# Late modulation in other groups and its sums four groups later; second half of the first modulation ahead of the first product

## The reference

```python
def adaln(cond, w, b):
    m = jax.nn.silu(cond) @ w + b
    return jnp.split(m, 6, axis=-1)

def trunk_block(x, mods, g1, g2, w1, w2, mixer):
    sh1, sc1, gt1, sh2, sc2, gt2 = mods
    mixed, ctx_tensors = mixer(modulate(rmsnorm(x, g1), sh1, sc1))
    x = x + gt1 * mixed
    hh = modulate(rmsnorm(x, g2), sh2, sc2)
    x = x + gt2 * (jnp.square(jax.nn.relu(hh @ w1)) @ w2)
    return x, ctx_tensors
```

## Time and profile before

| | us |
|---|---|
| median of 3 runs | 3748.66 |
| lowest and highest | 3743.83 to 3749.55 |
| the profiled execution | 3761.44 |
| its span, first to last instruction | 3760.1 |
| PE busy | 3568.7 (95%) |
| DVE busy | 2162.0 (57%) |
| mean granted clock of PE | 0.975 |

### The profile page before, as it was taken

How to read it: one execution, slowest core, us unless ns; L and a number is a source line. 1 busy time by engine, 2 the same in 40 slices (tenths; PEclk the granted TensorE clock), 3 DMA queues, 4 the chain that set the end, 5 groups by cost and what they waited for, 6 DMA issues and landing times. The chain is left out here.

```text
span 3760.1 us, 48494 instructions
## 1 busy us (share of the span) xinstructions
PE 3568.7 (95%) x19302; PEld 2735.7 (73%) x19302; DVE 2162.0 (57%) x3366; ACT 793.3 (21%) x1275; POOL 1072.2 (29%) x718
## 2 busy tenths in 40 slices
PE   7989999889999999999989999998899999999997
PEld 5887444447888888888868864444588888888886
DVE  6555676654656666666573247765446555455555
ACT  3111454441200000000031125544321000000003
POOL 0110577752211111111131127778231111111113
PEclk9999999999999999999999999999999999999999
DMA  6665344434112211211215454344501011111111
GB/s 233 192 206 167 81 122 113 126 100 172 51 66 53 79 58 61 79 50 69 69 56 162 157 145 108 84 129 114 186 32 57 25 44 45 34 34 45 34 34 56
DMA packets 274121, 350.50 MB, mean 93 GB/s; under 512 B 73286, under 2 KB 200472, under 8 KB 273768
## 3 DMA queue, kind: packets, MB, share of 16 engines
q1 hardware_dynamic: 240880, 332.75, 28.5%
q10 hardware_dynamic: 33016, 14.64, 1.9%
HBM read 280.00 MB, written 72.16 MB: 94 GB/s over the span
## 5 line engine op out<-in xcount | busy, mean ns | idle before, releaser
L2530 PE MATMUL bank<-h_hi,w_hi 128*128 128x512 f32 (+1 forms) x2496 | 904.8, 363 | 26.1 <-issue 10.5
L2531 PE MATMUL bank<-h_lo,w_hi 128*128 128x512 f32 (+1 forms) x2496 | 889.8, 356 | 0.0
L2532 PE MATMUL bank<-h_hi,w_lo 128*128 128x512 f32 (+1 forms) x2496 | 889.5, 356 | 0.0
L2345 DVE SCALAR_TENSOR_TENSOR xT<-bank,mods,xT 128x512 f32<-128x512 f32 (+1 forms) x816 | 534.3, 661 | 266.6 <-PE bank L2532 254.6
L2530 PE MATMUL bank<-m_hi,w_hi 128*128 128x512 f32 (+1 forms) x1536 | 554.4, 361 | 18.9 <-DVE xT L2345 18.6
L2530 PEld LDWEIGHTS bank<-h_hi,w_hi 128*128 128x128 f32 x2496 | 475.5, 190 | 102.0 <-issue 20.2
L2531 PE MATMUL bank<-m_lo,w_hi 128*128 128x512 f32 (+1 forms) x1536 | 548.2, 357 | 0.0
L2532 PE MATMUL bank<-m_hi,w_lo 128*128 128x512 f32 (+1 forms) x1536 | 548.1, 357 | 0.0
L2531 PEld LDWEIGHTS bank<-h_lo,w_hi 128*128 128x128 f32 x2496 | 475.7, 191 | 72.8 <-issue 5.3
L2532 PEld LDWEIGHTS bank<-h_hi,w_lo 128*128 128x128 f32 x2496 | 475.3, 190 | 67.8
L955 POOL TENSOR_SCALAR w_hi<-stage 128x2048 fp32r<-128x2048 f32 x90 | 174.2, 1935 | 1052.3 <-issue 527.6
(11 more groups left out here) (226 smaller groups left out, 4193.4 us busy)
## 6 DMA issues: line engine op xcount, KB each, us to landing
stage<-in_w_mlp SPq DMA_DIRECT2D x64, 1024.0 KB, 5.2
nx_w<-in_w_ada SPq DMA_DIRECT2D x16, 1536.0 KB, 9.4
stage<-in_w_in SPq DMA_DIRECT2D x18, 1024.0 KB, 6.2
late_w<-in_w_ada SPq DMA_DIRECT2D x32, 512.0 KB, 4.7
rope_t<-in_k_rope SPq DMA_DIRECT2D x28, 512.0 KB, 5.0
rden<-s_rden ACTq DMA_DIRECT2D x28, 320.0 KB, 4.6
ada_w<-in_w_ada SPq DMA_DIRECT2D x4, 2048.0 KB
stage<-in_w_out SPq DMA_DIRECT2D x8, 1024.0 KB, 6.4
```

What stands on the lines that cost most here:

```text
L2345: dve.scalar_tensor_tensor(out=x, in0=bank[:, bk, :n], scalar=mods[l][:, gate + k, cd:cd + 1], in1=x, op0=ALU.mult, op1=ALU.add).then_inc( ...
L2530: x = pe.matmul(out, a_hi, b_hi, start=first, stop=False)
L2531: pe.matmul(out, a_hi, b_lo, start=False, stop=False)
L2532: return x, pe.matmul(out, a_lo, b_hi, start=False, stop=last)
```

## The change

Five edits:

- LATE_GROUPS: the portions now follow groups 12 to 23, 28 to 30, 35 to 37 and 38 to 51. Before they followed groups 12 to 22 (11 portions) and 38 to 59 without 49 (21 portions).
- LATE_SUM_AT: the sums of four portions stand four groups behind the fourth one, at groups 19, 23, 27, 39, 43, 47, 51 and 55. Before they stood two turns behind it, at 17, 21, 40, 44, 48, 53, 57 and 61.
- LATE_END = 56: `late_mods` moves from group 60 to 56, and with it POOL's split of unit 8 (to 56) and DVE's (to 57).
- PE makes `rows(2)`, `rows(3)`, `columns(2)` and `columns(3)` before the first group.
- ACT's `copy_rows(2)` and `copy_rows(3)` stand ahead of h_hi for k = 3 and k = 4.

```diff
--- before.py
+++ after.py
@@ -554,8 +554,14 @@
             CACHE_AT[-1]: 8}
 LOAD_AT[0] = {0: 2, 10: 3, 15: 4, U_GROUPS[3][4]: 5, U_GROUPS[4][4]: 6, U_GROUPS[5][4]: 7, U_GROUPS[6][5]: 8}
 LATE_PARTS = 4 * (NADA - NADA1)
-LATE_AT = {g: r for r, g in enumerate(sorted([U_GROUPS[1][-1]] + U_GROUPS[2] + [U_GROUPS[4][-1]] + U_GROUPS[5] + U_GROUPS[6]))}
-assert len(LATE_AT) == LATE_PARTS
+LATE_GROUPS = list(range(12, 24)) + [28, 29, 30, 35, 36, 37] + list(range(38, 52))
+LATE_AT = {g: r for r, g in enumerate(LATE_GROUPS)}
+LATE_SUM_AT = {LATE_GROUPS[4 * n + 3] + 4: n for n in range(NADA - NADA1)}
+LATE_END = max(LATE_SUM_AT) + 1
+assert len(LATE_AT) == LATE_PARTS and LATE_END < CACHE_AT[-1]
+for _t, _g in ((HI_AT, LATE_END), (LO_AT, LATE_END + 1)):
+    _t[0] = {i: u for i, u in _t[0].items() if u != NU_IN - 1}
+    _t[0][_g] = NU_IN - 1
 
 
 Temps = namedtuple("Temps", "sq xr std rstd total")
@@ -1706,8 +1712,8 @@
 
             if l == 0:
                 for k in range(KT):
-                    if k in (2, 4):
-                        copy_rows(k // 2 + 1)
+                    if k in (3, 4):
+                        copy_rows(k - 1)
                     upper_norm(act, 0, 0, k)
             for k in range(KT):
                 upper_norm(act, l * 2, 1, k)
@@ -2112,7 +2118,7 @@
                     dve.wait_ge(rp_2, l * NR + r + 1 + CREDIT)
                     dve.tensor_tensor(zr[0], rp1, rp2[r % 2], ALU.add).then_inc(zr_rdy, 1)
                     lower(p, zr[0], 1.0)
-                if l == 0 and g["i"] == CACHE_AT[-1]:
+                if l == 0 and g["i"] == LATE_END:
                     late_mods()
                 if g["i"] in LO_AT[l]:
                     lo_unit(dve, l, LO_AT[l][g["i"]], unit_slot(LO_AT[l][g["i"]], l))
@@ -2581,11 +2587,6 @@
                             first.then_inc(w_used, 1)
                         if k == KT - 1:
                             mm.then_inc(z_full, 1)
-                    if l == 0 and g["c"] == 0 and k in (1, 3):
-                        rows(k // 2 + 2)
-                        if k == 3:
-                            columns(2)
-                            columns(3)
 
             def in_group(g):
                 i = g["i"]
@@ -2644,9 +2645,14 @@
                                        stop=True)
                 mm.then_inc(nx_sum, 1)
 
+            if l == 0:
+                for q in range(2, NADA1):
+                    rows(q)
+                for q in range(2, NADA1):
+                    columns(q)
             for g in GROUPS:
-                if l == 0 and LATE_AT.get(g["i"] - 2, 0) % 4 == 3:
-                    late_sums(LATE_AT[g["i"] - 2] // 4)
+                if l == 0 and g["i"] in LATE_SUM_AT:
+                    late_sums(LATE_SUM_AT[g["i"]])
                 if l and g["i"] == 2:
                     sum_all(pe, l * 2, 2)
                 if l and g["i"] == 3:
```

## The result

| | before | changed |
|---|---|---|
| median of the runs, us | 3749.55 (3743.83 to 3757.27, 5 runs) | 3731.57 (3727.45 to 3732.47, 5 runs) |
| ratio to before | | 0.9942, 95% interval 0.9928 to 0.9956 |
| the profiled execution, us | 3761.44 (span 3760.1) | 3729.83 (span 3728.4) |

The change makes the kernel faster by 0.58%. By this ratio some 22 us of the median of before are saved, by its interval 16 to 27; the two medians in the table lie 18.0 us apart. The forecast was 3729 us (3719 to 3740).

The account below looks back on a forecast made before the run. TensorE, busy 95% of the span, was taken as the bound, so time is won only where it stands or runs at low clock. 6.8 + 6 + 7 = 19.8 us, taken from the median 3748.66, gave 3728.9 us, range 3719 to 3740.

Parts of the forecast that it names:

- Term A: First modulation's second half, moved ahead of the first product: group 4 starts at 73.6 against 80.35, 6.8 us saved.
- `rows(3)` runs 44.8 to 46.7, two `columns` of 1.05 us end at 48.8: First modulation: row product takes 1.90 us once its weights land, so the first product starts at 48.8, 8.1 us later.
- low clock over more than 7 us behind 48.8: Start of the first product: seeing TensorE's low clock last this long would show the forecast wrong.
- Term B: Portions of groups 12 to 23, sums four groups behind: group 24 starts earlier, 6 us saved, bounds 4 to 7.3.
- Rotary stretch: Groups 23, 28 to 30, 35 to 37: seven portions moved here cost TensorE nothing; uncovered they would cost 21 us.
- rival (3): Rotary groups: seven late loads hold SyncE's queue, delaying tables and stores; with 5 us each 15 slower, 3764; chance 0.05.
- Term C: Groups 38 to 60: shorter portion chain lets group 61 start at 311.3 instead of 317.0; 7 us saved, 3 to 11.
- 13 more at 4.10: Groups 38 to 51: after portion 18 ends at 241.2, the remaining portions take 4.10 us each, ending at 294.5.
- The fifth sum: Sum of portions 16 to 19: expected to have the longest wait before a sum, about 5 us.
- rival (2): Late portions: freed of TensorE's stalls, the chain runs at 3.6 us per portion; 26.8 us saved, 3721.9; chance 0.10.
- Rival (1): Late sums: the stall returns because the portions' chain sets the pace, 4.5 us; 9.3 us saved, 3739.4; chance 0.15.
- Rival (4): First modulation doesn't gain, from late weights or cold starts; 13 to 16 us saved, 3734; chance included in forecast's 0.70.

Follow-up runs that it names:

- e1: The kernel before with only the second half of the first modulation (rows, columns, ScalarE's row copies) moved ahead of the first product; 3740.45 us, ratio 0.9978.
- e5: The changed kernel with TensorE's gaps before rows(2) and rows(3) filled by 9 and 14 products that nothing reads; 3731.92 us, ratio 0.9947.
- e8: The changed kernel with the sums five groups behind the last portion of their set instead of four; 3727.76 us, ratio 0.9939.
- e9: The changed kernel with the sums six groups behind the last portion of their set instead of four; 3728.47 us, ratio 0.9946.
- e3: The changed kernel with the sums back at two groups behind, so of the late part only the portions' groups are new; 3753.98 us, ratio 1.0010.
- e7: The changed kernel loading only 128 of 512 columns of each portion from portion 2 on, the rest made from old data; 3723.51 us, ratio 0.9925.

## Why the forecast was right, step by step

**The total** was right: 19.8 us saved were forecast; the ratio gives some 22, the medians 18.0, and the barrier of the profiles 23.0. Taking the sum from the median and not from the profiled run, which lay 12.8 us above it, was right too: behind the barrier that run took 3357.6 us, and the twelve other profiles 3350 on the mean, so most of the excess seems to lie there. That the parts came out so near owes something to luck: A was forecast 3.3 us too large for this profile and one sum was left out, while B and C were forecast 2.2 and 4.2 too small.

**Term A, 6.8 us forecast (3.9 to 9.1): mechanism right, size wrong in the changed kernel's profile (3.5).** `rows(3)` started at 45.49 (forecast 44.8), but the step "`rows(3)` runs 44.8 to 46.7, two `columns` of 1.05 us end at 48.8" failed: at half clock (0.50) they lasted until 52.59. I had allowed one slow stretch and put it into the product; it lay over both row products, the columns and the first quarter of the product (12 of 48 matmuls), 17.1 us in all. With low clock until 57.9 one of the forecast's own signs of being wrong came, "low clock over more than 7 us behind 48.8". The low end of 3.9 was too high for that. The second profile of the same kernel has 4.6 us, e1 7.0, and e5 with PE kept busy 7.6, where z_lo of group 1 is the next limit. A gap did not bring the low clock at once, nor every time: in the changed kernel the burst behind the gap of 2.31 us began at full clock, which fell 0.8 us later (40.85), and in e8 `rows(3)` ran at full clock (1.00) behind a gap of 2.08 us.

**Term B, 6 us forecast (4 to 7.3): too small.** Group 24 starts at 147.99, before at 159.64 (the forecast had 159.8): 11.7 us earlier, and without the 3.5 of term A 8.2. The forecast had worked out 7.3 and then took 6, for the case that portion 7 is no earlier than the 151.6 of before. That case did not come. Portion 7 ended at 144.89, which with the 3.5 us of term A is 148.4 on the forecast's time axis, where 150 had been assumed. The first sum waited 2.44 us (forecast 1.8). The second did not wait at all, where 147.2 to 150 had been reckoned, also because PE came to it only at 149.4 on that axis, after 3.4 us of low clock behind the first.

**Rotary stretch, nothing: right for the portions, but a sum was left out.** From group 23's cache turn to group 30's PE takes 33.31 us, of which 1.84 are the sum of portions 8 to 11, which before stood later; without it 31.47, before 31.53 (159.29 to 190.82). The seven loads and their portions cost PE nothing there, so rival (3) had no place to begin. The sum's 1.84 us no term had: the lead falls from 11.7 us at group 24 to 9.9 at group 37. Also right was that PE stands some 4 us near group 40 for z_lo of group 36: in the changed kernel the sum's wait of 4.14 us hides it, e9 shows it.

**Term C, 7 us forecast (3 to 11): too small.** From group 37's cache turn (9.9 us early) to group 62 (21.1 early) it gave 11.2, just over the upper bound. The wrong step is "13 more at 4.10": they took 3.76 each, and portion 31 ended at 280.32, which is 290.2 on the forecast's axis where 294.5 was reckoned. Of these 4.2 us 2.8 arrived at group 61, since PE came to the last sum only at 281.93 and was then the limit itself. Another 1.4 is the low clock of group 61, which went entirely (2.7), where I had counted half. The fifth sum, for which I forecast the longest wait (about 5 us), waited for nothing, and the waits came to 11.1 in place of 15 to 20. Up to 2.5 of the 11.2 us may be the difference between two executions, since e1 gained as much here with the code of before.

**Behind group 62** another 1.9 us came that no term had: before, a stretch of 3.4 us at half clock stood at 390.9; the changed kernel has none between group 62 and the barrier. So 3.5 + 8.2 - 1.7 + 11.2 + 1.9 gives the barrier's 23.0 within rounding.

**What moves the pace** is only in part shown. For portions 18 to 31 it was 4.10, 3.91 and 4.25 us in the three profiles with sums two groups behind (before, e1, e3), and 3.68 to 3.83 in the nine with four or more and full loads: there closer sums go with slower loads. For portions 2 to 11 no such split exists: e1 has 3.91 with PE standing 7.4 us, e9 3.98 with no sum that waits, e5 4.06, the changed kernel 3.78 and 3.79. So the fall from 4.10 to 3.78, on which term B's extra gain rests, has no cause shown.

**The rivals.** The truth lies between the forecast and rival (2), the chain that runs at its own pace. Its 3.6 us was worked out from a landing of 3.8, the least one; with the median landing of 4.5, 0.4 for the issue and the 2.73 us that four DVE operations take, the same sum gives 3.8, near the 3.76 measured. Rival (1), a pace of 4.5, went the wrong way. Rival (4), no gain from the modulation, did not happen: e1 is 8 us faster alone.

## What to carry to other kernels

Where one engine consumes what a slower chain of loads delivers, move the consumer away from the last producer by the chain's lateness in the consumer's own work, and look which wait stands right behind it: here four groups took out half of the waits, six groups all of them, and the next limit (z_lo of group 36) gave the time back. A wait that names a chain need not come from its loads: the longest one left here came from a store, two engines away. Reckon the pace of such a chain from the median landing and as a range, for the same loads (portions 2 to 11) went at 3.7 to 4.1 us each in profiles whose waits do not explain it. A wait of TensorE is to be priced with the low clock behind it: here waits of 2.31 and 2.58 us were followed by 17.1 us at half clock, one of 2.42 by 6.8 and one of 2.44 by 3.4, half of which is lost where TensorE works.

## What the hardware showed that I had not expected

How long the granted clock stays at half (0.50) behind the same wait in the same code differs between executions: behind a wait of 2.1 to 2.7 us ahead of `rows(2)` it was low for 17.1 us in the changed kernel and in e7, for 10.2 in e9, for 3.4 and then 10.2 us in the second profile of the changed kernel, and for 3.4 us in e8. Filling the gaps with 23 unused matmuls (e5) kept the clock at full there, 1.00 from 40 to 60 us. A load of a quarter of the size (128 KB for 512 KB) landed in 2.2 us where the full one took 4.5: half the time, not a quarter.
